# MLP products of a row tile in another order in each of four projections, in a two-layer hybrid encoder step on one core

## What is computed

```python
def squared_relu_mlp(xn, w_up, w_down):
    h = jax.nn.relu(xn @ w_up)
    return (h * h) @ w_down
...
        x = x + y.astype(x.dtype)
        x = x + cross_attend(rmsnorm(x, p['norm_cross'][l]), mem_k[l], mem_v[l], p['x_wq'][l], p['x_wo'][l])
        x = x + squared_relu_mlp(rmsnorm(x, p['norm_mlp'][l]), p['mlp_w_up'][l], p['mlp_w_down'][l])
```

## Time and profile before

| | |
|---|---|
| device time, median of 3 runs | 2212.45 us (2211.91 to 2214.03) |
| the profiled execution, first to last instruction | 2209.8 us |
| TensorE busy, matmuls | 2157.6 us, 98% |
| TensorE busy, weight loads | 2019.4 us, 91% |
| VectorE / GpSimd / ScalarE busy | 57% / 53% / 19% |
| matmuls, weight loads | 15817, 15817 |
| read from and written to device memory | 200.05 MB, 33.89 MB |

### The profile page before, as it was taken

How to read it: one execution, slowest core, us unless ns; L and a number is a source line. 1 busy time by engine, 2 the same in 40 slices (tenths; PEclk the granted TensorE clock), 3 DMA queues, 4 the chain that set the end, 5 groups by cost and what they waited for, 6 DMA issues and landing times. The chain is left out here.

```text
span 2209.8 us, 38815 instructions
## 1 busy us (share of the span) xinstructions
PE 2157.6 (98%) x15817; PEld 2019.4 (91%) x15817; DVE 1260.4 (57%) x2091; ACT 416.9 (19%) x768; POOL 1173.1 (53%) x1119
## 2 busy tenths in 40 slices
PE   8999999999999999999999999999999999999997
PEld 8988889989999999999999995587699999999997
DVE  6988984454625343676557645772754364436263
ACT  5223451322000000121202113431322220000001
POOL 7564556526665665666657650032254466656653
PEclk9999999999999999999999999999999999999999
DMA  6224245202222222223433323552331122222221
GB/s 218 77 81 145 101 149 201 72 33 88 77 77 96 76 76 93 77 92 144 160 139 141 141 100 139 199 195 77 120 143 68 39 89 84 77 85 87 76 95 43
DMA packets 38330, 235.84 MB, mean 107 GB/s; under 512 B 4528, under 2 KB 7600, under 8 KB 12856
## 3 DMA queue, kind: packets, MB, share of 16 engines
q1 hardware_dynamic: 21600, 154.15, 19.7%
q10 hardware_dynamic: 16600, 79.80, 9.5%
HBM read 200.05 MB, written 33.89 MB: 106 GB/s over the span
## 5 line engine op out<-in xcount | busy, mean ns | idle before, releaser
L470 POOL TENSOR_TENSOR wlo<-raw,whi 128x512 fp32r<-128x512 f32 x580 | 797.4, 1378 | 134.0 <-ACT whi L1139 91.3
L466 POOL TENSOR_SCALAR whi<-raw 128x512 fp32r<-128x512 f32 x512 | 367.3, 717 | 838.0 <-PE psum L555 777.9
L555 PE MATMUL psum<-xnh,whi 128*128 128x288 f32 (+1 forms) x2816 | 615.1, 296 | 19.6 <-DVE xnl L1666 8.2
L555 PE MATMUL psum<-xnh,wlo 128*128 128x288 f32 (+1 forms) x2816 | 611.2, 295 | 0.0
L555 PE MATMUL psum<-xnl,whi 128*128 128x288 f32 (+1 forms) x2816 | 610.8, 295 | 0.0
L555 PEld LDWEIGHTS psum<-xnh,whi 128*128 128x128 f32 x2816 | 457.6, 189 | 27.1 <-issue 19.9
L555 PEld LDWEIGHTS psum<-xnl,whi 128*128 128x128 f32 x2816 | 457.4, 189 | 0.0
L555 PEld LDWEIGHTS psum<-xnh,wlo 128*128 128x128 f32 x2816 | 457.4, 189 | 0.0
L555 PE MATMUL psum<-hh,whi 128*128 128x288 f32 x1024 | 218.8, 295 | 2.1 <-DVE hl L2209 2.1
L555 PE MATMUL psum<-hl,whi 128*128 128x288 f32 x1024 | 218.9, 294 | 0.0
L555 PE MATMUL psum<-hh,wlo 128*128 128x288 f32 x1024 | 217.3, 293 | 0.0
(11 more groups left out here) (438 smaller groups left out, 2687.5 us busy)
## 6 DMA issues: line engine op xcount, KB each, us to landing
raw<-in_w SPq DMA_DIRECT2D x146, 1024.0 KB, 4.7
C<-in_C ACTq DMA_DIRECT2D x4, 1024.0 KB, 4.8
o_cp<-mvt ACTq DMA_DIRECT2D x4, 1024.0 KB, 4.1
o_cs<-C ACTq DMA_DIRECT2D x4, 1024.0 KB, 6.6
t_xc<-xc ACTq DMA_DIRECT2D x3, 1152.0 KB, 7.3
t_z<-mv ACTq DMA_DIRECT2D x3, 1152.0 KB, 4.2
t_q<-mq ACTq DMA_DIRECT2D x3, 1152.0 KB, 4.2
t_k<-mk ACTq DMA_DIRECT2D x3, 1152.0 KB, 4.2
```

The source lines that it names most:

```text
L466: pool.tensor_scalar(whi[:, s, c], raw[:, s, c], 1.0, 1.0, ALU.mult, ALU.mult).then_inc(S("slab_hi"), 1)
L470: ins = pool.tensor_tensor(wlo[:, s, c], raw[:, s, c], whi[:, s, c].bitcast(F32), ALU.subtract)
L555: ins = pe.matmul(bank(g, 2 * m + b)[:, 0:t1 - t0], W[wi][:, kk, m0 + m, :], r[:, kk, t0:t1], start=(at_first and wi == 0 and r is rh), st ...
```

## The change

`project` takes a list `turns` that holds the order of the twelve matmuls of a row tile as triples (column tile m, part p, token half b). Without it the order is the one of before. `mlp` passes such a list, one for the up and one for the down slabs of each layer:

- up, layer 0: m, then b, then p innermost (the token half outside the parts)
- up, layer 1: b, then m, then p innermost (the token half outermost)
- down, layer 0: p, then b, then m innermost (the column tiles innermost)
- down, layer 1: m, then b, then p innermost

`slab_begun` goes up with the matmul (0, 0, 1), column tile 0, part 0, second token half: the 4th of the slab in up of layer 0 and down of layer 1, the 7th in up of layer 1, the 3rd in down of layer 0. Each bank is still started by its part 0 of the first row tile and ended by its part 2 of the last. The first up slab of each layer keeps its order.

```diff
             def project(g, n, rh, rl, kts=DT, m0=0, ms=2, wait=None, turn=None, first=True, halves=((0, HALF), (HALF, T)),
-                        order=None, start=True, stop=True, close=True, tiles_freed=False, columns=(0, 1), half=False):
+                        order=None, start=True, stop=True, close=True, tiles_freed=False, columns=(0, 1), half=False,
+                        turns=None):
...
-                    for m in columns:
-                        for wi, r in ((0, rh), (0, rl), (1, rh)):
-                            for b, (t0, t1) in enumerate(halves):
-                                ins = pe.matmul(bank(g, 2 * m + b)[:, 0:t1 - t0], W[wi][:, kk, m0 + m, :], r[:, kk, t0:t1],
-                                                start=(at_first and wi == 0 and r is rh), stop=(at_last and wi == 1))
-                            if first and kk == order[0] and m == 0 and wi == 0 and r is rh:
-                                ins.then_inc(S("slab_begun"), 1)
+                    parts = ((0, rh), (0, rl), (1, rh))
+                    for m, p, b in turns or [(m, p, b) for m in columns for p in range(3) for b in range(len(halves))]:
+                        (wi, r), (t0, t1) = parts[p], halves[b]
+                        ins = pe.matmul(bank(g, 2 * m + b)[:, 0:t1 - t0], W[wi][:, kk, m0 + m, :], r[:, kk, t0:t1],
+                                        start=at_first and p == 0, stop=at_last and p == 2)
+                        if first and kk == order[0] and (m, p, b) == (0, 0, len(halves) - 1):
+                            ins.then_inc(S("slab_begun"), 1)
...
             def mlp(l):
                 g0, n0 = GR["mlp", l, 0, "up", 0], SL["mlp", l, 0, "up", 0]
+                two = range(2)
+                up = ([(m, p, b) for m in two for b in two for p in range(3)],
+                      [(m, p, b) for b in two for m in two for p in range(3)])[l]
+                down = ([(m, p, b) for p in range(3) for b in two for m in two],
+                        [(m, p, b) for m in two for b in two for p in (0, 1, 2)])[l]
...
-                            project(g0 + i, n0 + i, xnh, xnl, turn=tn is not None and (tg, tn) or None)
+                            project(g0 + i, n0 + i, xnh, xnl, turn=tn is not None and (tg, tn) or None, turns=up)
...
                         project(g0 + 4 + i, n0 + 4 + i, hh, hl, turn=tn is not None and (tg, tn) or None,
-                                wait=hid if i == 0 else None)
+                                wait=hid if i == 0 else None, turns=down)
```

## The result

| | before | changed |
|---|---|---|
| device time, median of 20 runs each | 2212.24 us (2207.83 to 2214.92) | 2216.32 us (2214.86 to 2219.22) |
| profiled execution, first to last instruction | 2209.8 us | 2213.1 us |

What follows compares the result with a forecast made beforehand. The prediction took TensorE's own pace, busy 98% of the span, as the bound. Its only nonzero term was +2.6 us in layer 1's up slabs, on 2212.45 us: 2215.0 us, ratio 1.0012, range 2203 to 2219.

Steps and rivals of the forecast that it cites:

- the first rival: Everything falls to 133.3 ns a matmul, down slabs too: +5.4 us, 2217.9 us; chance 0.28.
- TensorE's pace is all that counts: Whole kernel: TensorE busy 98% of the span, so only its own pace and few waits can move the time.
- Up, layer 0: 0: Layer 0's 15 reordered up slabs: 133.3 ns a matmul before and after, so 0.
- The estimate from the 256- and 512-column streams: Parts-innermost streams carry 13.3 ns over their columns; for 288 columns that gives 133.3 ns a matmul.
- Up, layer 1: +2.6 us: Layer 1's up slabs: eight go from 130.0 to 133.3 ns a matmul, seven stay at 133.3; +2.6 us.
- The fast pace is a rhythm that is entered: Matmul stream: pace, such as 130.0 ns, is a rhythm kept once entered, depending on entry and on tiles read.
- Down: 0: Down slabs of both layers stay at 132.2 ns a matmul: 0, bounds +2.8 and -5.4 us.
- the row of the same tiles: Down slabs: trace reading of 132.2 ns on these tiles in all eight quarters, chosen over 133.3 ns.
- The wait: 0 +- 0.1 us a slab: Each quarter's first down slab: wait for the last hidden tiles, about 0.43 us, stays; change 0 +- 0.1 us per slab.
- the later signal: slab_begun comes 0.13 to 0.67 us later, delaying GpSimd's split; over 4 us of cover, so 0.
- a rival in which order could not matter: Nothing moves: the eight fast slabs find their rhythm again, the kernel stays at 2212.5 us; chance 0.09.

Runs made afterwards that it cites:

- all_parts_inner: Changed kernel with one order everywhere in the MLP (column tile, token half, parts innermost); 2217.68 us in one run.
- before_again: The kernel before, unchanged, run and traced once more; 2213.72 us in one run.
- hh_shifted: Kernel before, orders kept, with 64 bytes left free ahead of the hidden tiles hh and hl; 2212.8 us in one run.
- changed_shifted: Changed kernel, its four orders kept, with xnh and xnl 64 bytes further on; 2208.42 us (median of 11 runs), ratio 0.9985 to the kernel before.
- signal_second: Changed kernel with slab_begun back on the second matmul issued in a slab, orders kept; 2214.89 us in one run.
- low_last: Kernel before, but in each quarter's first down slab row tiles 6 and 7 do high hidden products first, eight low ones last; 2206.53 us, ratio 0.9979.

## Why the prediction was right, and where it was not

The time, 2216.3, lies 1.3 us above the forecast of 2215.0 and between it and the first rival (2217.9). By mechanism, too, the result stands between the two. Of the +4.3 us in the MLP 1.8 came from layer 1's up slabs, where the forecast put all of its +2.6; the other 2.6 came from two terms that it had at 0. Point by point:

1. **TensorE's pace is all that counts; shares and counts don't move.** Right.
2. **Up, layer 0: 0.** Right, 12.80 before and after. The estimate from the 256- and 512-column streams held there to 0.01 us a slab, and in all_parts_inner for layer 1 too. But a flat 13.3 ns over the columns is no rule for parts innermost: the same order took 12.69 on hidden tiles, and with the half outermost 12.75 on normed ones. That the estimate held owes something to the place of `xnh` and `xnl`.
3. **Up, layer 1: +2.6 us.** The mechanism was right, the eight fast slabs were lost; the term was mis-sized. They went to 12.75 and not 12.80 (+2.1), and the seven slow ones went there too (-0.4): +1.8 us measured. The forecast's count of eight came from one execution; before_again also had eight, in other quarters, so in that count there was luck. I had read the half-outermost order as just another form with parts innermost.
4. **The fast pace is a rhythm that is entered.** Right, and the runs showed more than the prediction dared: before_again had it in other quarters, hh_shifted showed it being handed from one kind of slab to the next. That it would not come back under the new orders was a choice among rows; in the seven kernels with new orders in the up slabs no MLP up stretch was at 12.48, each seen in one execution, and one of them, changed_shifted, at a place where the old order had none either.
5. **Down: 0.** This step failed for layer 0. I took "the row of the same tiles" and let order go for nothing. Layer 1's order with parts innermost did keep 12.69, but column tiles innermost took 12.80 on hidden tiles wherever it ran: +1.3 us. Order and place both count. The first rival had this pace right for layer 0 and wrong for layer 1.
6. **The wait: 0 +- 0.1 us a slab.** Mis-sized: +0.13 us in layer 0 and +0.15 in layer 1 at the start of row tile 6; with the pace of the 24 matmuls behind it that is the +1.3 us of the eight slabs. I had put the later signal down as covered, because TensorE does not need the split for another 4 us. That cover is real, no slab start waits. But GpSimd's split runs beside VectorE's chain, and the chain is what TensorE waits for. The prediction named this route and allowed 0.1 us for it, on either side; the runs gave more, and to one side. That the pace of the first 72 matmuls is swallowed by the wait held: in layer 0 of signal_second they run slower than before and row tile 6 starts 0.02 us later.
7. **The rule on two independent read ports.** The Trainium skill, TensorE: Matmul & The Clock Gate, Step-by-step: what each phase is for, says that one port feeds the streaming operand and another the weights. From that the prediction drew a rival in which order could not matter. Here one form at one clock took 12.48 to 12.92 us a slab by order and place, so order does matter; whether the two ports meet anywhere no run shows.

Steps 5 and 6 together are +2.6 us, step 3 is 0.8 less than forecast (1.8 for 2.6): 2.6 + 2.6 - 0.8 = 4.4 us, but for rounding the whole of the MLP's +4.3 in the ledger, against 4.1 measured by the medians. That the total was close owes something to luck: the errors have opposite signs, and of the down slabs, which the first rival had slower throughout, one layer moved and the other did not.

What stays open: why 64 bytes matter, and what in the entry decides between 12.48 and 12.80. The runs show that place and order decide; no run moved the weights against a multiple of 128 bytes or changed the banks alone, so whether it is the reading of the moving operand, its place relative to the weights or the writing of the sums is open.

## What to carry to other kernels

Where one engine is busy for 98%, read the step between starts of the same form over long stretches, slab by slab and in more than one execution, before any argument on order: two paces of one form are worth more than a rule. Vary the tiles' places in steps of 32 and 64 bytes before reordering matmuls for their pace: here no new order gained time, and moving two tiles by 64 bytes took the changed kernel from a ratio of 1.0019 to 0.9985. It can also lose: at 32 and 96 no slab was at 12.48 or 12.69. The order that did gain, low_last, took a wait off the path. And a signal that seems to have microseconds of cover still moves the work behind it against whatever runs on the engine next to it.

## What the runs showed of the hardware

Numbers are for 128x288 fp32r matmuls, each with its own weight load, at granted clock 1.00; start to start is the slab's length over 96. Left out are slabs with a wait and the second up slab of a layer, whose second matmul starts 0.27 us after its first in every kernel looked at. Most entries rest on one execution each, of one or a few kernels.

| order of the twelve (outer to inner) | tile at 0 of 128 bytes | at 64 | at 32 or 96 |
|---|---|---|---|
| column tile, part, half (before) | 12.80 or 12.48 | 12.69 | 12.80 |
| column tile, half, part | 12.80 | 12.69 | not run |
| half, column tile, part | 12.75 | 12.75 or 12.69 | not run |
| part, half, column tile | 12.84 to 12.91 | 12.80 | not run |
| column tile, part, half turning back | 12.87 to 12.92 | not run | not run |

Between 130.0 and 134.6 ns a matmul, then, for the same work. VectorE's cast and subtraction of 128x288 and GpSimd's pieces stretch each other: the four subtractions took 2.94 us beside the end of a split and 4.10 us where they met more of it, the four casts 2.48 to 3.56 us by where the split lay, the last `whi` piece of GpSimd 0.67 and 0.83 us.
